# First block: the third query unit projected before the compressed keys' unit, and fewer weight units made ready at three early steps

## The chip, the cores and the metric

The program runs on one core of a Trainium2 chip. The metric is the device time of one execution in microseconds (us), as the median of several executions. The engines are TensorE (PE in the rows, its weight loads PEld), VectorE (DVE), ScalarE (ACT), GpSimd (POOL) and SyncE (SP), which issues nearly all DMAs.

## The reference

Two stacks of two layers each, on 256 tokens of width 1024. The change touches only the first stack, whose layer normalizes, projects into many pieces, runs three mixers, and then a feed-forward part:

```python
for l in range(DEPTH):
    h = rms_norm(x, ln1_gain[l])
    proj = h @ w_in[l]
    (nsa_q, k_cmp, v_cmp, k_slc, v_slc, k_win, v_win, nsa_gate,
     mla_cq, mla_ckv, mla_kpe, ret_q, ret_k, ret_v, ret_gate) = jnp.split(proj, offsets, axis=-1)
    o_nsa = nsa_mixer(partial_rope(nsa_q), partial_rope(k_cmp), v_cmp, partial_rope(k_slc), v_slc,
                      partial_rope(k_win), v_win, nsa_gate, ...)
    o_mla = mla_mixer(mla_cq, mla_ckv, mla_kpe, ...)
    o_ret = retention_mixer(ret_q, ret_k, ret_v, ret_gate, ...)
    x = x + concatenate([o_nsa, o_mla, o_ret]) @ w_out[l]
    x = x + square(relu(rms_norm(x, ln2_gain[l]) @ w_up[l])) @ w_down[l]
```

Inside `nsa_mixer` the compressed keys and values come from windows of 32 tokens, flattened and sent through a two-layer product: `kc = gelu((blocks(k_cmp) + pos_k) @ w1_k) @ w2_k`, and the same for values. Six query heads attend to selected keys, to a window of keys and to the compressed ones.

## The kernel before

All weights stream from HBM as tiles of 1 MB (128 x 2048 floats) through a ring of four slots (`ring`). SP issues the loads in one fixed order; before the load of tile g it waits until tile g-4, the one in the same slot, is released. Most tiles hold two weight units of 128 x 1024. A unit is split before use: ACT copies it to a rounded high part `wH` (L1305) and DVE subtracts to get the low part `wL` (L1648). A tile of units is released by the second subtraction. There are four places for split units, so unit n can be made only after TensorE is done with unit n-4. `feed(count)` on ACT and on DVE makes ready all units up to a count, in order, and each engine stops in it until the tile has landed (ACT) or the high part is there (DVE). A unit's projection is 24 matmuls (three for each of 8 chunks, L763 to L765).

A few tiles are used whole and unsplit: `cmpk` and `cmpv` (the first weights of the compression) and `small` (weights of the latent attention and the second ones of the compression). `cmpk` is released when TensorE ends `hidk`, its product (L944, 16 matmuls with 30 columns, each run as two passes, hence x32), and `cmpv` by `hidv`.

The tiles of a layer of the first block begin: 0 (cq0, cq1), 1 (ckv, q0), 2 (ks, q1), 3 and 4 token-major units, 5 (kc, q2), 6 cmpk, 7 (kw, vc), 8 (kpe, rqa), 9 cmpv, 10 small, 11 (rka, rqb), 12 (rkb, r4), 13 and 14 token-major, 15 the output product. The names are column groups of `w_in`: q0, q1, q2 the query heads in pairs, ks, kw, kc the selected, window and compressed keys, vc the compressed values, kpe and the r's for the other mixers. Unit numbers run along: kc 10, q2 11, kw 12, vc 13, kpe 14, rqa 15, rka 16, rqb 17, rkb 18, r4 19. So tile 10 (small) takes the slot of cmpk and can be loaded only when hidk has run, and tile 11 with units 16 and 17 is issued behind it in SP's order.

After the first units come 19 steps (`SLOTS1`), in which attention heads and projections alternate. Step i holds, on each engine, in this order:

- TensorE: projection `FILL1[i]`, with the rotations `MID1[i]` (L854) in its middle; on even i the scores of heads i and i+1 (L870, L872); the transposes of the weights of head i-1 (L885); the values of head i-2 (L893 to L895); then `END1[i]`: hidk, hidv, latent keys mk0 to mk4 (L974, from tile small), and so on.
- VectorE: rotary embeddings of `MID1[i]` (L1765 to L1771), behind kc's also four shifted copies and four additions of positions (L1873 to L1885), on which hidk waits; then `feed(fed_by(i))`; the row maxima of head i's scores (L1780); the output of head i-2 (L1922 to L1929).
- ScalarE: `feed(fed_by(i))`; the copy of the projection out of PSUM (L1253); the copy of the transposes (L1353); the copies of `END1[i]`'s results; the exponentials of head i (L1345, L1347).

Scores of heads 4 and 5 (step 4) need q2 after its rotary embedding, and the row maxima up to head 3. Scores of heads 6 and 7 (step 6) need the maxima up to head 5. The order is written out by hand in the tables `UNITS1`, `FILL1`, `MID1` and `END1`; `fed_by(i)` follows from which units' readers lie before step i and gives 16 at step 4, then 17, 18, 19, 20 at steps 5 to 8.

Of the kernel before, what the change touches and what calls it, by code (L numbers as in the profile page):

```python
# [45 lines left out]
assert KC * 256 == TILE  # L46


UNITS1 = ["cq0", "cq1", "ckv", "q0", "ks", "q1", "kc", "q2", "kw", "vc", "kpe", "rqa", "rka", "rqb", "rkb", "r4"]
RAW1 = {u: 6 + i if i < 3 else (i - 3) % 6 for i, u in enumerate(UNITS1)}  # L50
UNITS2 = [f"q{b}" for b in range(4)] + [f"k{b}" for b in range(4)]
LATER2 = ["pa", "pb", "cua", "cub", "cba", "cbb", "cca", "ccb"]
# [31 lines left out]

PAIRS1 = [(UNITS1[2 * i], UNITS1[2 * i + 1]) for i in range(8)]
TILES1 = (
# [92 lines left out]
def down_steps(kf):  # L179

    out = []
    for n in range(KC):
# [4 lines left out]
    return out  # L187


FILL1 = ["tm10", "tm11", "kc", "q2", "kw", "vc", "kpe", "rqa", "rka", "rqb", "rkb", "r4", "tm20", "tm21", "tm30", "tm31"]  # L190
SLOTS1 = NH1 + 2
MID1 = {3: ["kc"], 4: ["q2"], 5: ["kw"], 7: ["kpe"], 8: ["rqa"], 9: ["rka", "mq0"], 10: ["rqb", "mq1"],
        11: ["rkb", "mq2"], 12: ["r4", "mq3"], 13: ["mq4"]}
ROPES1 = ["q0", "ks", "q1"] + [u for i in range(SLOTS1) for u in MID1.get(i, [])]
END1 = {4: ["hidk"], 6: ["mk0", "mk1", "mk2"], 7: ["hidv", "mk3", "mk4"], 8: ["mv0", "mv1", "mq0"], 9: ["mq1", "mq2"],
        10: ["kcc", "mq3", "mq4", "vbd"], 11: ["cs0", "cs1"], 12: ["rs0", "rs1"],
        13: ["ct", "ro0", "ro1", "rs2", "rs3"], 14: ["co0", "co1", "ro2", "ro3", "rs4"], 15: ["ro4"],
        16: ["mt0", "mt1"], 17: ["mt2"]}
# [3 lines left out]
def fill1(i):  # L202

    return FILL1[i] if i < len(FILL1) else None


def fed_by(i):

    done = UNITS1[:6] + ["tm00", "tm01"] + FILL1[:i]
    n = SPLIT  # L210
    while n - SPLIT < 24 and SU1[n - SPLIT][2] in done:
        n += 1
    return min(n, 22) if i == 11 else n


SIDE = 3
# [2 lines left out]
def order1():  # L219

    out = UNITS1[:SIDE] + ["ss1", "q0", "rot_q0", "ks", "rot_ks", "q1", "ssqk", "rot_q1", "tm00", "tm01"]
    for i in range(SLOTS1):
        out += ["rot_" + u for u in MID1.get(i, [])]
        out += [fill1(i)] if fill1(i) else []
        out += END1.get(i, [])
    out += [f"wo{n}" for n in range(KC)]
# [82 lines left out]
def norm1(l, second):  # L309

    return 2 * l + second
# [87 lines left out]
def trn_kernel(nc, consts, vec1, vec2, once, pos, xin, stream, out):  # L399
    ctx = ExitStack()  # L400
    with ctx:
# [328 lines left out]
        def _(pe):  # L730
# [53 lines left out]
            def project_side_by_side(names, ready, y):  # L784

                chunk = side_by_side(names, y)
                for c in range(KC):
                    ready(c)
                    chunk(c)

            def normed(base):

                return lambda c: pe.wait_ge(h_ready, state["layer"] * (2 * KC) + (base + c + 1))

            def project(name, y, mid=None, ready=None):

                wh, wl = blocks(next_unit())
                a = open_acc(name)
                for c in range(KC):
                    if ready is not None:  # L800
                        ready(c)
                    if mid is not None and c == KC // 2:
                        mid()
                    last = split_product(a[:, 0:S], (wh[:, c, :], wl[:, c, :]), y(c), c == 0, c == KC - 1)
                last.then_inc(acc_full, 1)
# [31 lines left out]
            def sum_squares(name, norm):  # L837

                both = norm == norm2(0, 0)
                a = open_acc(name)  # L840
                pe.wait_ge(sum_ready, norm + 1)
                pe.matmul(a[:, 0:S], one[:], tcs[:, 0, :] if both else sq[:, 3, :], start=True, stop=False)
                pe.wait_ge(sq_ready, SQUARES * (norm + 1))
                pe.matmul(a[:, 0:S], g7[:] if both else one[:], sq[:, KC - 1, :], start=False, stop=True)\
                    .then_inc(acc_full, 1)
                if both:

                    pe.wait_ge(plain_ready, 1)
                    pe.matmul(ps_o[:, 0:S], one[:], sq[:, 3, :], start=True, stop=False)
                    pe.matmul(ps_o[:, 0:S], one[:], sq[:, KC - 1, :], start=False, stop=True).then_inc(plain_full, 1)  # L850
# [65 lines left out]
            for L in range(LAYERS):  # L916
                enter(A1, L)

                def rotated(u):

                    if u[:2] == "mq":
                        mla_rotate(int(u[2]))
                        return
                    drained(u)
                    i = RAW1[u]
                    if u == "kpe":
                        rotate(u, C("rotm")[0:96, 0:96], raw[0:96, i, :], slice(0, 96))
                    else:
                        rotate(u, C("rotr" if u[0] == "r" else "rotp"), raw[:, i, :])
# [136 lines left out]
                def after(i):  # L1066

                    for name in END1.get(i, []):
                        n = int(name[-1]) if name[-1].isdigit() else None
# [18 lines left out]
                def middle(i):  # L1088

                    for u in MID1.get(i, []):  # L1090
                        rotated(u)

                if L == 0:
                    for n, u in enumerate(UNITS1[:SIDE]):
                        project(u, hs, ready=normed(0) if n == 0 else None)
                    pe.wait_ge(one_ready, 1)
                    pe.wait_ge(early_in, 16 * 2)
                else:
                    project_side_by_side(UNITS1[:SIDE], normed(0), hs)
                sum_squares("ss1", norm1(L, 0))  # L1100
# [129 lines left out]
        def _(act):  # L1230
# [133 lines left out]
            for L in range(LAYERS):  # L1364
# [61 lines left out]
                def taken_after(i):  # L1426

                    for name in END1.get(i, []):
                        n = int(name[-1]) if name[-1].isdigit() else None
# [53 lines left out]
                for c in range(IN_TURN, HEADS_DONE):  # L1483
                    mixed_high(c)
                feed(fed_by(NH1))
                for c in range(HEADS_DONE, KC):
                    mixed_high(c)
# [90 lines left out]
        def _(dve):  # L1578
# [206 lines left out]
            for L in range(LAYERS):  # L1785
# [27 lines left out]
                def scaled(tables, by):  # L1813

                    n = len(range(4)[tables])
                    t = trig[:, :, tables, :]
                    link(TTN(t, t, by.unsqueeze(1).unsqueeze(1).to_broadcast([P, 2, n, S]), ALU.mult))
# [28 lines left out]
                def rope1_block(u):  # L1846

                    dve.wait_ge(acc_drained[A1.bank(u)], A1.drained(u, L))
                    allr = slice(0, P)
                    src = None if u[:2] == "mq" else raw[:, RAW1[u], :]  # L1850
                    done = L * len(ROPES1) + ROPES1.index(u) + 1
                    if u[:2] == "mq":
                        hh = int(u[2])
                        rope(A1, u, L, qm[64:96, hh, :], 1, [(qm[64:96, hh, :], slice(64, 96))], rope_ready, slice(64, 96))
                    elif u == "kpe":
                        rope(A1, u, L, src[64:96, :], 1, [(km[64:96, 0, :], slice(64, 96))], rope_ready, slice(64, 96))
                        dve.wait_ge(rope_ready, done)
                        nc.vector.tensor_copy(km[64:96, 1:5, :], km[64:96, 0:1, :].to_broadcast([32, 4, S]))\
                            .then_inc(km_ready, 1)
                    elif u == "kc":  # L1860
                        rope(A1, u, L, src, 0, [(nt, allr)], rope_ready)
                        dve.wait_ge(rope_ready, done)
                        shifted(nt, 0)
                    elif u == "r4":
                        rope(A1, u, L, src, 2, [(rope1[0:64, 9, :], slice(0, 64)), (rope1[0:64, 10, :], slice(64, 128))],
                             rope_ready)
                    else:
                        rope(A1, u, L, src, 2 if u[0] == "r" else 0, [(rope1[:, ROPE1[u], :], allr)], rope_ready)
# [197 lines left out]
                for i in range(SLOTS1):  # L2066
# [5 lines left out]
                    if (L, i) == (0, 7):  # L2072
                        dve.wait_ge(trig_ready, 4)
                        scaled(slice(2, 3), rn[:])
                    for u in MID1.get(i, []):
                        rope1_block(u)
                    if i == 6:
                        shifted(raw[:, RAW1["vc"], :], 1)
                    if i < NH1 - 1:
                        feed(fed_by(i))  # L2080
# [32 lines left out]
                    if i == 17:  # L2113
                        dve.wait_ge(o_drained, L * NH1 + (NH1 - 1) + 1)
                        dve.sem_inc(mla_ready, 1)
                    for name in END1.get(i, []):
                        if name[:2] == "mt":
# [383 lines left out]
```

## Time and profile before

| | |
|---|---|
| timed runs | 1563.92, 1570.98, 1573.01 us; median 1570.98 us |
| profiled execution | 1560.0 us, of which 1558.2 us are the span of the engines' work |
| PE busy | 1487.5 us, 95% of the span |
| DVE busy | 1086.7 us, 70% |
| ACT busy | 783.7 us, 50% |
| DMA | 296.51 MB, 190 GB/s on average |
| chain that ended last | PE 77%, DVE 12%, DMA 4%, ACT 3% |

The profile is of one execution. Its steps 0 to 18 of the first layer lie at about 45 to 190 us, of the second layer at about 417 to 545 us. A matmul row's idle time stands in brackets with the releaser. The granted clock of TensorE has two levels, 2.4 GHz (1.00) and 1.2 GHz (0.50); a mean in between is a stretch with both.

### The profile page before, as it was taken

What the parts mean: (1) busy time and instruction counts of PE and PEld (TensorE: products, weight loads), DVE (VectorE), ACT (ScalarE), POOL (GpSimd) and SP (SyncE); (2) the same over time, 40 slices, a digit from 0 to 9 for tenths busy, and PEclk for the clock granted to TensorE, in tenths of its full rate; (3) what the DMA queues carried; (4) which work ended last, traced back from release to release, by engine and by line L of the source; (5) the groups of instructions that cost most, each with busy time, mean ns of one, the idle gap of its engine ahead of it and who ended that gap; (6) DMA issues with size and microseconds to landing.
All of it is one profiled execution on the core that took longest, in us unless ns stands there. A gap on an engine that the chain in (4) does not pass through costs nothing.

```text
span 1558.2 us, 28765 instructions
## 1 busy us (share of the span) xinstructions
PE 1487.5 (95%) x11878; PEld 1444.9 (93%) x11878; DVE 1086.7 (70%) x1927; ACT 783.7 (50%) x1364; POOL 59.5 (4%) x61
## 2 busy tenths in 40 slices
PE   6899899999989899999899998999989999899999
PEld 5888899999988799999899988999989999799999
DVE  8658678888667678888985476666458746766653
ACT  6544567634534477733546545444435554454442
POOL 0000000000000000000030040000001202100000
PEclk9889999999999999999999999999999999999999
DMA  8123259898323149998544443555534444445552
GB/s 324 55 109 139 81 217 332 339 352 324 136 82 139 52 176 335 337 356 331 186 153 155 163 153 118 200 182 188 190 135 163 163 140 161 161 163 186 176 184 78
DMA packets 42433, 296.51 MB, mean 190 GB/s; under 512 B 5056, under 2 KB 5312, under 8 KB 6848
## 3 DMA queue, kind: packets, MB, share of 16 engines
q1 hardware_dynamic: 41888, 294.66, 51.5%
q8 instruction: 95, 1.56, 0.4%
q14 instruction: 34, 0.28, 0.1%
q10 hardware_dynamic: 416, 0.02, 0.0%
HBM read 293.61 MB, written 1.05 MB: 189 GB/s over the span
## 4 chain that ended last, share of the span: by engine, by line
PE 77%; DVE 12%; DMA 4%; ACT 3%; issue 2%; POOL 1%; SPq 0%; DVEq 0%; ACTq 0%
PE acc L763 23%; PE acc L765 22%; PE acc L764 22%; DVE wL L1648 4%; DMA ring<-stream 4%; ACT wH L1305 2%; PE acc L944 1%; PE ps_t L885 1%; PE acc L854 1%; PE ps_s L872 1%; PE ps_o L894 1%; PE ps_o L895 1%; PE ps_s L870 1%; PE acc L952 1%; POOL region L2361 1%
## 5 line engine op out<-in xcount | busy, mean ns | idle before, releaser
L1648 DVE TENSOR_TENSOR wL<-ring,wH 128x1024 fp32r<-128x1024 f32 x444 | 548.9, 1243 | 284.6 <-ACT wH L1305 279.7
L763 PE MATMUL acc<-hH,wH 128*128 128x256 f32 x2240 | 654.1, 292 | 33.6 <-DVE wL L1648 15.6
L764 PE MATMUL acc<-hL,wH 128*128 128x256 f32 x2240 | 639.0, 285 | 0.0
L765 PE MATMUL acc<-hH,wL 128*128 128x256 f32 x2240 | 638.8, 285 | 0.0
L1305 ACT ACTIVATE wH<-ring 128x1024 fp32r<-128x1024 f32 x444 | 463.7, 1051 | 229.7 <-DMA ring<-stream 118.1
L763 PEld LDWEIGHTS acc<-hH,wH 128*128 128x128 f32 x2240 | 435.2, 194 | 43.5 <-issue 25.5
L764 PEld LDWEIGHTS acc<-hL,wH 128*128 128x128 f32 x2240 | 435.4, 194 | 3.5 <-issue 2.6
L765 PEld LDWEIGHTS acc<-hH,wL 128*128 128x128 f32 x2240 | 434.9, 194 | 0.0
L763 PE MATMUL acc<-aH,wH 128*128 128x256 f32 x864 | 244.6, 283 | 0.0
L764 PE MATMUL acc<-aL,wH 128*128 128x256 f32 x864 | 244.5, 283 | 0.0
L765 PE MATMUL acc<-aH,wL 128*128 128x256 f32 x864 | 244.5, 283 | 0.0
L763 PEld LDWEIGHTS acc<-aH,wH 128*128 128x128 f32 x864 | 165.9, 192 | 0.1
L764 PEld LDWEIGHTS acc<-aL,wH 128*128 128x128 f32 x864 | 165.9, 192 | 0.0
L765 PEld LDWEIGHTS acc<-aH,wL 128*128 128x128 f32 x864 | 165.9, 192 | 0.0
L1253 ACT ACTIVATE region<-acc 128x256 f32<-128x256 f32 (+4 forms) x142 | 53.7, 379 | 192.5 <-PE acc L765 159.1
L1638 DVE SCALAR_TENSOR_TENSOR ring<-ring,onc 128x1024 f32<-128x1024 f32 x96 | 117.0, 1219 | 0.4 <-DMA ring<-stream 0.4
L763 PE MATMUL acc<-wH,hH 128*128 128x256 f32 (+1 forms) x192 | 58.3, 304 | 3.7 <-DVE tss L1767 1.5
L1780 DVE CUSTOM_DVE_ANT_0 weights<-ps_s,cst 128x128 f32<-128x128 f32 x100 | 31.3, 354 | 34.8 <-PE ps_s L872 34.4
L764 PE MATMUL acc<-wL,hH 128*128 128x256 f32 (+1 forms) x192 | 54.4, 283 | 0.0
L765 PE MATMUL acc<-wH,hL 128*128 128x256 f32 (+1 forms) x192 | 54.4, 283 | 0.0
L2348 POOL TENSOR_TENSOR region<-region 128x256 f32<-128x256 f32 x12 | 13.2, 1100 | 1069.8 <-ACT region L1253 1068.8
L763 PEld LDWEIGHTS acc<-wH,hH 128*128 128x128 f32 x192 | 37.1, 193 | 7.6 <-issue 4.3
(312 smaller groups left out, 1699.9 us busy)
## 6 DMA issues: line engine op xcount, KB each, us to landing
ring<-stream SPq DMA_DIRECT2D x276, 1024.0 KB, 4.9
cst<-consts SPq DMA_DIRECT2D x1, 1347.0 KB, 16.0
x<-xin SPq DMA_DIRECT2D x4, 256.0 KB, 3.8
out<-x SPq DMA_DIRECT2D x4, 256.0 KB, 4.2
onc<-once SPq DMA_DIRECT2D x1, 516.0 KB, 16.2
v1all<-vec SPq DMA_DIRECT2D x1, 355.0 KB, 9.7
v2all<-vec SPq DMA_DIRECT2D x1, 330.0 KB, 17.0
nv<-pos SPq DMA_DIRECT2D x1, 256.0 KB, 3.5
```

The lines of the kernel that those rows point to most:

```text
L763: pe.matmul(out, w[0], y[0], start=first, stop=False)
L764: pe.matmul(out, w[0], y[1], start=False, stop=False)
L765: return pe.matmul(out, w[1], y[0], start=False, stop=last)
L854: pe.matmul(a[rows, 0:S], m, src, start=True, stop=True).then_inc(acc_full, 1)
L870: pe.matmul(b[:, 0:P], q[:, 0:P], k[:, 0:P], start=True, stop=True)
L872: pe.matmul(b[:, P:3 * P], q[:, P:S], k, start=True, stop=True).then_inc(s_full, 1)
L885: last = pe.transpose(ps_t[:, c * P:(c + 1) * P], pr[:, j % 2, c * P:(c + 1) * P], C("ident"))
L1253: act.activation(dst, a[rows, 0:n], func, **kw).then_inc(acc_drained[tn.bank(name)], 1)
L1305: act.activation(wH[:, n % SPLIT, :], ring[:, g % RING, half * UNIT:(half + 1) * UNIT], ACT.Copy)\
L1638: STT(products, products, 1.0, cb2, ALU.mult, ALU.mult, accum_out=adac[:, 2 * j + half:2 * j + half + 1])\
L1648: TTN(wL[:, n % SPLIT, :], ring[:, g % RING, half * UNIT:(half + 1) * UNIT], wH[:, n % SPLIT, :].bitcast(F32), ALU.subtract).then_inc(lo_r ...
L1780: last = nc.vector.tensor_tensor_reduce(sm[:, i % 2, cols], ps_s[i % 2][:, cols], C("mask")[:, cols], -scale, FLT_MAX, ALU.add, ALU.min, n ...
```

## The change

Three tables swap q2 and kc, and hidk goes from the end of step 4 to the end of step 5. The two units change halves in tile 5 and their numbers (q2 is unit 10, kc unit 11). DVE now makes q2's rotary embedding at step 3 and kc's with its copies at step 4. `fed_by` is capped at steps 5, 6 and 7, so that unit 16 isn't made at step 5 nor unit 17 at step 6, but both at step 7; steps 4 and 8 and the later ones reach the same counts as before. Nothing is added to or removed from the work.

```diff
-UNITS1 = ["cq0", "cq1", "ckv", "q0", "ks", "q1", "kc", "q2", "kw", "vc", ...]
+UNITS1 = ["cq0", "cq1", "ckv", "q0", "ks", "q1", "q2", "kc", "kw", "vc", ...]
...
-FILL1 = ["tm10", "tm11", "kc", "q2", "kw", ...]
+FILL1 = ["tm10", "tm11", "q2", "kc", "kw", ...]
...
-MID1 = {3: ["kc"], 4: ["q2"], 5: ["kw"], ...}
+MID1 = {3: ["q2"], 4: ["kc"], 5: ["kw"], ...}
...
-END1 = {4: ["hidk"], 6: ["mk0", "mk1", "mk2"], ...}
+END1 = {5: ["hidk"], 6: ["mk0", "mk1", "mk2"], ...}
...
+FED_AT_MOST = {5: 16, 6: 16, 7: 18, 11: 22}
...
-    return min(n, 22) if i == 11 else n
+    return min(n, FED_AT_MOST.get(i, n))
```

Lines of the changed program lie 3 further on. VectorE, from step 3's rotary embedding on (first layer), before: kc's embedding (into `nt`), copies and additions, then the unit's split.

```order
L1765 TENSOR_TENSOR tcs<-region,trig 128x256
L1767 TENSOR_TENSOR tss<-acc,trig 128x256
L1771 TENSOR_TENSOR nt<-tcs,tss 128x256
L1873 COPY region<-nt 64x256
L1874 COPY region<-nt 64x255
L1875 COPY region<-nt 64x255
L1876 COPY region<-nt 64x256
L1884 TENSOR_TENSOR region<-region,v1all 128x8x15
L1885 TENSOR_TENSOR region<-region,v1all 128x8x15
L1884 TENSOR_TENSOR region<-region,v1all 128x8x15
L1885 TENSOR_TENSOR region<-region,v1all 128x8x15
L1648 TENSOR_TENSOR wL<-ring,wH 128x1024
```

The same place in the changed program: q2's embedding, the split, head 3's maxima (L1783), head 1's output, and then kc's embedding.

```order
L1768 TENSOR_TENSOR tcs<-region,trig 128x256
L1770 TENSOR_TENSOR tss<-acc,trig 128x256
L1774 TENSOR_TENSOR region<-tcs,tss 128x256
L1651 TENSOR_TENSOR wL<-ring,wH 128x1024
L1783 ISA weights,nmax<-ps_s,cst 128x128
L1783 ISA nmax 128x1
L1783 ISA weights,nmax<-ps_s,cst 128x256
L1783 ISA nmax 128x1
L1925 RECIPROCAL coef<-psumv 128x2
L1928 TENSOR_TENSOR coef<-coef,region 128x2
L1932 TENSOR_TENSOR region<-ps_o,coef 128x2x64
L1768 TENSOR_TENSOR tcs<-region,trig 128x256
```

The eight copies and additions moved behind step 3's maxima and output, and behind q2's embedding.

ScalarE from the end of step 4 on, before: hidk's copy (128x30), head 4's exponentials, the split of unit 16, then step 5's transposed copy and exponentials, the split of unit 17, step 6's copies.

```order
L1253 ACTIVATE region<-acc 128x30
L1345 ACTIVATE weights,psumv<-weights,nmax 128x128
L1347 ACTIVATE weights,psumv<-weights,nmax 128x256
L1305 ACTIVATE wH<-ring 128x1024
L1353 ACTIVATE weights<-ps_t 128x384
L1345 ACTIVATE weights,psumv<-weights,nmax 128x128
L1347 ACTIVATE weights,psumv<-weights,nmax 128x256
L1305 ACTIVATE wH<-ring 128x1024
L1353 ACTIVATE weights<-ps_t 128x384
L1253 ACTIVATE region<-acc 64x256 x3
```

The same stretch in the changed program, from head 4's exponentials to step 7's split of two units:

```order
L1348 ACTIVATE weights,psumv<-weights,nmax 128x128
L1350 ACTIVATE weights,psumv<-weights,nmax 128x256
L1356 ACTIVATE weights<-ps_t 128x384
L1256 ACTIVATE region<-acc 128x30
L1348 ACTIVATE weights,psumv<-weights,nmax 128x128
L1350 ACTIVATE weights,psumv<-weights,nmax 128x256
L1356 ACTIVATE weights<-ps_t 128x384
L1256 ACTIVATE region<-acc 64x256 x3
L1348 ACTIVATE weights,psumv<-weights,nmax 128x128
L1350 ACTIVATE weights,psumv<-weights,nmax 128x256
L1308 ACTIVATE wH<-ring 128x1024 x2
```

hidk's copy went one step later, and both splits to step 7, behind step 6's exponentials.

## Rows read from the trace of the kernel before

**Rows 1.** The page: TensorE's busy time, and the chain that ended last by engine.

```profile
PE 1487.5 (95%) x11878; PEld 1444.9 (93%) x11878; DVE 1086.7 (70%) x1927; ACT 783.7 (50%) x1364; POOL 59.5 (4%) x61
PE 77%; DVE 12%; DMA 4%; ACT 3%; issue 2%; POOL 1%; SPq 0%; DVEq 0%; ACTq 0%
```

**Rows 2.** The chain in order of time, first layer: start, duration, what.

```profile
61.67 0.42 DVE tcs L1765
...
62.92 0.28 DVE region L1873
...
65.32 1.13 DVE wL L1648
66.45 0.20 DVE weights L1780
...
67.11 0.17 DVE coef L1925
...
67.60 0.33 DVE tcs L1765
...
78.37 0.33 SPq L695
...
85.64 1.07 ACT wH L1305
```

**Rows 3.** Timeline of TensorE, first layer: start, duration, form, idle time and releaser.

```profile
68.78 0.49 PE L870 MATMUL ps_s<-region 64*128 64x128 f32 x4 [2.44 <-DVE region L1771]
...
71.36 6.98 PE L944 MATMUL acc<-region,ring 128*128 128x30 f32 x32
...
88.66 0.49 PE L870 MATMUL ps_s<-region 64*128 64x128 f32 x4 [0.68 <-DVE nmax L1780]
...
90.68 1.51 PE L974 MATMUL acc<-region,ring 128*64 128x256 f32 x6
...
94.60 0.64 PE L854 MATMUL acc<-region,cst 96*96 96x256 f32 x2 [0.78 <-DVE region L1842]
```

**Rows 4.** Stretches, first layer: PE, PEld, DVE, ACT, POOL busy, granted clock, DMA.

```profile
66.00:71.40 5.40, 2.96 (x21) 2.43 (x20) 4.64 (x18) 2.69 (x7) 0.00 (x0) 0.86 0.00 0
71.40:78.20 6.80, 6.80 (x34) 6.80 (x33) 0.62 (x2) 0.00 (x0) 0.00 (x0) 0.50 0.00 0
78.20:86.00 7.80, 7.80 (x45) 7.62 (x46) 0.85 (x2) 1.44 (x6) 0.00 (x0) 0.66 0.87 327
...
97.50:104.00 6.50, 6.50 (x40) 5.28 (x39) 2.50 (x9) 1.08 (x5) 0.00 (x0) 0.74 0.19 53
104.00:110.00 6.00, 6.00 (x39) 5.36 (x37) 2.23 (x6) 2.12 (x6) 0.00 (x0) 0.72 0.30 122
```

**Rows 5.** Timeline of TensorE, second layer.

```profile
438.44 0.49 PE L870 MATMUL ps_s<-region 64*128 64x128 f32 x4 [1.09 <-DVE region L1771]
...
440.30 3.71 PE L944 MATMUL acc<-region,ring 128*128 128x30 f32 x32
443.84 0.37 PE L763 MATMUL acc<-hH,wH 128*128 128x256 f32 x1
...
448.14 0.37 PE L763 MATMUL acc<-hH,wH 128*128 128x256 f32 x1
...
454.33 0.49 PE L870 MATMUL ps_s<-region 64*128 64x128 f32 x4 [3.07 <-DVE nmax L1780]
...
463.76 3.71 PE L944 MATMUL acc<-region,ring 128*128 128x30 f32 x32
```

**Rows 6.** Stretches, second layer, columns as in rows 4.

```profile
454.00:460.00 6.00, 5.67 (x28) 4.01 (x29) 5.75 (x23) 3.56 (x10) 0.00 (x0) 0.72 0.00 0
```

**Rows 7.** Timeline of ScalarE: exponentials, first layer; the split of unit 16, second layer.

```profile
67.44 0.49 ACT L1347 ACTIVATE weights<-weights,nmax 128x256 f32<-128x256 f32 x1
...
451.31 1.06 ACT L1305 ACTIVATE wH<-ring 128x1024 fp32r<-128x1024 f32 x1 [6.20 <-DMA ring<-stream]
```

**Rows 8.** Line L695 (loads) from 76 to 90 us, three loads: issue to landing.

```profile
DMA to landing us min/median/max: 4.7/6.9/10.3
```

More of the change, by code:

```diff
@@ L46 @@
 assert KC * 256 == TILE
-UNITS1 = ["cq0", "cq1", "ckv", "q0", "ks", "q1", "kc", "q2", "kw", "vc", "kpe", "rqa", "rka", "rqb", "rkb", "r4"]
+UNITS1 = ["cq0", "cq1", "ckv", "q0", "ks", "q1", "q2", "kc", "kw", "vc", "kpe", "rqa", "rka", "rqb", "rkb", "r4"]
 RAW1 = {u: 6 + i if i < 3 else (i - 3) % 6 for i, u in enumerate(UNITS1)}
@@ L187, in down_steps @@
     return out
-FILL1 = ["tm10", "tm11", "kc", "q2", "kw", "vc", "kpe", "rqa", "rka", "rqb", "rkb", "r4", "tm20", "tm21", "tm30", "tm31"]
+FILL1 = ["tm10", "tm11", "q2", "kc", "kw", "vc", "kpe", "rqa", "rka", "rqb", "rkb", "r4", "tm20", "tm21", "tm30", "tm31"]
 SLOTS1 = NH1 + 2
-MID1 = {3: ["kc"], 4: ["q2"], 5: ["kw"], 7: ["kpe"], 8: ["rqa"], 9: ["rka", "mq0"], 10: ["rqb", "mq1"],
+MID1 = {3: ["q2"], 4: ["kc"], 5: ["kw"], 7: ["kpe"], 8: ["rqa"], 9: ["rka", "mq0"], 10: ["rqb", "mq1"],
         11: ["rkb", "mq2"], 12: ["r4", "mq3"], 13: ["mq4"]}
 ROPES1 = ["q0", "ks", "q1"] + [u for i in range(SLOTS1) for u in MID1.get(i, [])]
-END1 = {4: ["hidk"], 6: ["mk0", "mk1", "mk2"], 7: ["hidv", "mk3", "mk4"], 8: ["mv0", "mv1", "mq0"], 9: ["mq1", "mq2"],
+END1 = {5: ["hidk"], 6: ["mk0", "mk1", "mk2"], 7: ["hidv", "mk3", "mk4"], 8: ["mv0", "mv1", "mq0"], 9: ["mq1", "mq2"],
         10: ["kcc", "mq3", "mq4", "vbd"], 11: ["cs0", "cs1"], 12: ["rs0", "rs1"],
```

## The prediction

> **What bounds the kernel now.** I first read the page. TensorE is busy for 95% of the span and holds 77% of the chain that ended last [rows 1], so nearly everything else is hidden. A change in order can only give back what TensorE loses: time in which it stands still, and time in which it runs at the lower clock. So I looked in TensorE's timeline at steps 3 to 8 of both layers for the idle times in brackets, and in the stretches for the granted clock.
>
> First layer. At step 4 TensorE stands still for 2.44 us before the scores of heads 4 and 5, released by q2's rotary embedding [rows 3]. The chain shows why that is late: VectorE makes kc's embedding from 61.67, its copies and additions from 62.92, the split from 65.32, head 3's maxima from 66.45 and head 1's output from 67.11, and begins q2's embedding only at 67.60 [rows 2]. After this stop the clock is at 1.2 GHz for some 14 us: the product hidk takes 6.98 us [rows 3], where in the second layer, at 2.4 GHz, it takes 3.71 [rows 5]. When hidk ends at 78.37, SP issues the load of small and behind it that of tile 11; ScalarE, at step 5's split of unit 16, stands until tile 11 has landed, 85.64 [rows 2]. The maxima of head 5 wait behind that, and TensorE waits 0.68 us for them, then 0.78 for the next VectorE result [rows 3]. That is short only since the slow clock stretched its own work. A second stretch at the lower clock lies at 97.5 to 110 [rows 4].
>
> Second layer. The same two places: 1.09 us for q2, without a fall of the clock behind it, and 3.07 us for head 5's maxima [rows 5], behind a split that waited 6.20 us for its tile [rows 7]; then the clock fell [rows 6].
>
> **What the change moves, part by part.** The work is the same; I walk through the steps with its measured lengths.
>
> *q2 before kc.* VectorE's pieces are: an embedding 62.92 - 61.67 = 1.25 us, copies and additions 65.32 - 62.92 = 2.40, split 1.13, maxima 67.11 - 66.45 = 0.66, output 67.60 - 67.11 = 0.49 [rows 2]. New order from 61.67: q2 embedded at 62.92, split 64.05, head 3's maxima 64.71, output 65.20. TensorE asks for the scores at 68.78 - 2.44 = 66.34, and both of their conditions are met by 64.71. The stall is gone, with 1.6 us to spare. In the second layer it asks 1.09 us before 438.44, and q2's embedding moves up there by as much as here, 67.60 - 61.67 = 5.9 us. Gain 2.44 + 1.09.
>
> *What is late next on VectorE.* kc's embedding and copies now stand ahead of head 4's maxima: 65.20 + 1.25 + 2.40 + 1.13 + 0.66 = 70.64, and the exponentials on ScalarE end 67.44 + 0.49 - 67.11 = 0.82 us behind their maxima [rows 7], at 71.5. TensorE: scores, transposes and values take 440.30 - 438.44 = 1.86 us [rows 5], so vc's projection starts at 66.34 + 1.86 = 68.20. A whole odd step (projection with rotation, transposes, values) takes 448.14 - 443.84 = 4.30; I estimate transposes and values at half of the 1.86, 0.9 us, so it wants head 4's weights at 68.20 + 3.4 = 71.6. That is a tie: I take 0, and 0.3 us as the bound. Kc's additions are done at 68.85, long before hidk.
>
> *hidk one step later.* It starts at 68.20 + 4.30 = 72.50 and, at the full clock, ends at 72.50 + 443.84 - 440.30 = 76.04, where before it ended at 78.37. In the second layer it ends 3.0 us later than before (437.35 + 1.86 + 4.30 + 3.54 = 447.05, against 444.04), but with vc's step already behind it.
>
> *The small tile.* This is the new danger. The three latent keys at the end of step 6 read tile small, which now has one step less to land. After hidk TensorE has kpe's projection, 454.33 - 3.07 - 448.14 = 3.12 us, then scores, transposes and values, 1.86: 4.98 us in all. The first of the three loads landed 4.7 us after its issue [rows 8], and SP issues it at once. So the tile is there 0.2 us early: cost 0. The bound above is the landing of the second load, 6.9, which would be 2 us in each layer.
>
> *Units 16 and 17 at step 7.* ScalarE and VectorE no longer stop at step 5 for tile 11, so head 5's maxima are made early, and the stops of 0.68 and 3.07 us go; VectorE also has vc's and kpe's copies out of PSUM in time, so 0.78 goes. At step 7 ScalarE gets to the split at about 4.98 + 1.5 (mk0 to mk2 [rows 3]) = 6.5 us after hidk's end and may wait until 6.9 + 0.3; TensorE needs unit 16 only at step 8, that is after an odd step's 4.3, hidv's 3.7 [rows 5] and two latent keys' 1.0, some 9 us on. Two splits in step 7 and two in step 8 hold VectorE for 2.3 us each. Cost 0, hidden under hidv; without that cover it would be one split, 1.13 us.
>
> *The clock.* What a stretch loses is its length times (1 - clock). First layer, the fall after the first stop: 5.40 x 0.14 + 6.80 x 0.50 + 7.80 x 0.34 = 6.81 us; the second one: 6.50 x 0.26 + 6.00 x 0.28 = 3.37 us [rows 4]. Second layer: 6.00 x 0.28 = 1.68 us [rows 6]. The first and the third stand right behind a stop of 2.44 and 3.07 us that goes away, so I count them as gained. The second stands in and behind hidv, whose matmuls have only 30 columns, after stops of 0.68 and 0.78 us. The hidv of the second layer shows no fall. The trace doesn't decide it: I leave this fall where it is, and keep 0 and 3.37 as ends.
>
> The Trainium skill (TensorE: Matmul & The Clock Gate, Part 1) says that the check behind the clock runs freely and isn't tied to the kernel's start, so that the point of a change varies from run to run. Of the three such products that began at the full clock, one had a fall and two had none, which agrees. That rule makes the rival below on falls at each of these products.
>
> **The sum.** First layer 2.44 + 0.68 + 0.78 + 6.81 = 10.71; second layer 1.09 + 3.07 + 1.68 = 5.84; together 16.55 us, all of it on TensorE's own path. Later work moves up with it, since every load waits for a slot and not for a point in time. Against the profiled execution: 1560.0 - 16.6 = 1543.4. That execution is 11 us under the median of the timed runs, so the forecast is set against the median: 1570.98 - 16.55 = **1554.4 us**. The gap may be falls of the clock that the profiled execution was spared, for instance behind the stop of 1.09; then the gain is larger.
>
> **Rivals.** *All falls go* (0.20): the fall at hidv goes with the stops before it, 16.55 + 3.37 = 19.9 us, 1551.1. For it: the undisturbed hidv of the second layer.
>
> *Falls at the narrow products* (0.20): hidk now runs at the full clock in both layers and may pull it down, as hidv did. If all four do so at 3.37 us each, the gain is 19.9 - 13.5 = 6.4 us, 1564.6; with two or three, 1558 to 1561. Against it: two of the three that began at the full clock have no fall, and the one in the first layer had two stops before it.
>
> *Only the swap works* (0.05): the block on ScalarE shows up again at step 7 and TensorE stops for it as at step 6 before. What is left is the gain of step 4, 2.44 + 1.09 + 6.81 = 10.3 us, 1560.6. Against it: the 9 us of work that lie between.
>
> *small is late by 2 us* (0.07): it lands as the second load did. That is a stop of 1.9 us in each layer and, as after 2.44 us before, one fall of 6.8: 16.55 - 3.8 - 6.8 = 5.9, 1565.1.
>
> *Slower* (0.03): the three loads issued together share the engines so that small lands last, at 10.3 [rows 8]. TensorE then stops 5.3 us in each layer, with a fall of 6.8 behind it: 16.55 - 24.2 = -7.7, 1578.7. It turns to a loss when stop and fall together pass 8.3 us a layer. Against it: in the rows the first load lands first.
>
> The Trainium skill (DMA: Bandwidth & Descriptors, Queues, rings and completion order) says that completion isn't first-in first-out for one issuing engine, which is the rule by which this rival would come about. The landings of 4.7, 6.9 and 10.3 us do not show it.
>
> **Chances and range.** The forecast itself has 0.45. Half a per cent, 7.9 us, is about what a measurement of this kernel can tell from no change. Under 1563.1 lie the forecast, the first rival, 0.14 of the second and most of the third: faster 0.84. The rest is within (0.13), and 0.03 slower. The range goes from the best case, 1551.1, less 5 us for the scatter of the timed runs (9 us between lowest and highest), to the second rival's end: 1546 to 1565.
>
> **What would show it.** In the changed kernel's rows: no idle time before the scores of step 4 in either layer; hidk 3.7 us long in both; no wait of ScalarE for its tile at step 5; at most some tenths before mk0 (L977, then with DMA as releaser); mk0 starting near 81.0 in the first layer instead of 90.68, and in the second hidv starting 10.7 + 5.8 = 16.5 us earlier than 463.76. A stop at step 5's transposes would mean that kc's chain is too long for its new place; a stop at mk0 that small is the new bound; a clock of 0.50 behind hidk without a stop, the second rival.

## The result

Seven executions of each kernel on one chip gave a median of 1549.04 us for the changed kernel (1544.11 to 1550.31) and 1559.62 us for the kernel before (1557.81 to 1573.01; the three shown ahead of the prediction are among them). The ratio is 0.9898, 95% interval 0.9875 to 0.9921: faster by 1.0%, 10.6 us. The profiled execution of the changed kernel took 1549.25 us, 10.8 us less than the profiled one of before. The forecast was a gain of 16.6 us and a time of 1554.4 us. One of the ten executions of the swap alone, a variant further down, took 3661.84 us and is in none of its figures.

TensorE's timeline of the changed kernel, first layer from step 4 to the latent keys (start, duration, form; an idle time would stand in brackets at the end):

```profile
67.14 0.49 PE L873 MATMUL ps_s<-region 64*128 64x128 f32 x4
...
72.55 0.52 PE L888 MATMUL ps_t<-cst,weights 128*128 128x128 f32 x3
...
73.53 4.98 PE L947 MATMUL acc<-region,ring 128*128 128x30 f32 x32
...
83.22 0.49 PE L873 MATMUL ps_s<-region 64*128 64x128 f32 x4
...
85.17 1.51 PE L977 MATMUL acc<-region,ring 128*64 128x256 f32 x6
...
90.95 3.71 PE L947 MATMUL acc<-region,ring 128*128 128x30 f32 x32
```

None of the stops of [rows 3] is left. The scores of step 4 follow without one, those of step 6 (83.22) too, and the latent keys (85.17, before 90.68) find their tile. Step 5's transposes (72.55) carry no bracket; they start 0.3 us behind the start of the matmul ahead of them, against 0.1 us in the second layer, so the tie cost 0.2 us at most. But hidk, forecast at 3.7 us in this view, takes 4.98. The second layer shows the same:

```profile
428.67 0.49 PE L873 MATMUL ps_s<-region 64*128 64x128 f32 x4
...
434.83 4.53 PE L947 MATMUL acc<-region,ring 128*128 128x30 f32 x32
...
444.50 0.49 PE L873 MATMUL ps_s<-region 64*128 64x128 f32 x4
...
452.23 3.71 PE L947 MATMUL acc<-region,ring 128*128 128x30 f32 x32
```

The stops of 1.09 and 3.07 us of [rows 5] are gone. The stretches say what happened to hidk (PE, PEld, DVE, ACT, POOL busy, granted clock, DMA share, GB/s):

```profile
66.00:75.70 9.70, 9.66 (x83) 8.97 (x81) 9.31 (x35) 3.65 (x10) 0.00 (x0) 1.00 0.00 0
75.70:82.50 6.80, 6.80 (x33) 6.80 (x33) 1.15 (x5) 1.06 (x5) 0.00 (x0) 0.50 0.43 154
...
434.00:437.50 3.50, 3.50 (x35) 3.50 (x33) 3.15 (x15) 0.49 (x1) 0.00 (x0) 1.00 0.02 5
437.50:444.30 6.80, 6.80 (x34) 6.80 (x33) 0.63 (x3) 1.06 (x5) 0.00 (x0) 0.50 0.59 204
```

TensorE was busy for all but 0.04 us of the stretch before, and yet the clock fell to 1.2 GHz within hidk (at 75.7 and 437.5 us), in both layers, for 6.8 us each: half of that, 3.4 us a layer, was lost. Of the falls of before [rows 4, 6], the one behind the first stop and the one at hidv are gone, as is the one of the second layer's step 6.

Two further stretches fell in this execution that had not in the one of before. Where the second layer starts, TensorE waits a little shorter than before (2.04 us, before 2.58), and the clock falls:

```profile
378.32 0.36 PE L766 MATMUL acc<-hH,wH 128*128 128x256 f32 x1 [2.04 <-DVE tss L2176]
```

At the start of the second block it falls at 744.7 us, behind a stop of 2.66 us that is the same in both kernels. Both kernels reach this stop with the same work, so I count this fall as chance and not as the change's.

### The profile page after: what moved, and what is told of

Read it like the earlier page. It is cut to its first block, busy times and chain, and to the rows that moved or that the text cites. A ratio compares the mean times of both kernels' runs of the same rounds, so it can differ in the third digit from the quotient of the medians.

```text
span 1547.4 us, 28765 instructions
## 1 busy us (share of the span) xinstructions
PE 1483.0 (96%) x11878; PEld 1441.1 (93%) x11878; DVE 1085.8 (70%) x1927; ACT 780.0 (50%) x1364; POOL 59.4 (4%) x61
## 4 chain that ended last, share of the span: by engine, by line
PE 68%; DVE 14%; DMA 10%; ACT 4%; issue 2%; POOL 1%; SPq 0%; DVEq 0%; ACTq 0%
PE acc L766 20%; PE acc L768 19%; PE acc L767 19%; DMA ring<-stream 10%; DVE wL L1651 6%; ACT wH L1308 3%; DVE ring L1641 2%; PE ps_t L888 1%; PE acc L947 1%; PE acc L857 1%; PE ps_s L875 1%; PE ps_o L897 1%; PE ps_o L898 1%; PE ps_s L873 1%; PE acc L955 1%
## 5 line engine op out<-in xcount | busy, mean ns | idle before, releaser
L1308 ACT ACTIVATE wH<-ring 128x1024 fp32r<-128x1024 f32 x444 | 461.7, 1050 | 232.3 <-DMA ring<-stream 130.6
L1783 DVE CUSTOM_DVE_ANT_0 weights<-ps_s,cst 128x128 f32<-128x128 f32 x100 | 31.3, 353 | 48.8 <-PE ps_s L875 48.4
```

The costliest lines, as they stand in the source:

```text
L1308: act.activation(wH[:, n % SPLIT, :], ring[:, g % RING, half * UNIT:(half + 1) * UNIT], ACT.Copy)\
L1783: last = nc.vector.tensor_tensor_reduce(sm[:, i % 2, cols], ps_s[i % 2][:, cols], C("mask")[:, cols], -scale, FLT_MAX, ALU.add, ALU.min, n ...
```

## The experiments

Four kernels ran on a second chip and four on a third, each time beside the kernel before. On those the kernel before has medians of 1566.9 us (29 executions, 1554 to 1577) and 1567.9 us (25 executions, 1555 to 1574). Each execution comes with its mean granted clock, so its time splits into lost clock, (1 - mean clock) x span, and the rest. (A stop that falls into a stretch at 1.2 GHz is put down by this to lost clock with half its length.) For the kernel before on the third chip that is 31.3 us lost and 1535.1 us rest on average; time and lost clock go together over its executions (correlation 0.82). By the scatter of these 25 (a standard deviation of 4.7 us), a median of three can lie 5 us off, by my estimate. Unless a 95% interval of a ratio is given, the intervals below are estimates from such standard deviations.

### Wider matmuls for hidk and hidv

```diff
+flat_f = fk[j].rearrange("p m g n -> p (m g n)")
 for m in range(16):
-    last = pe.matmul(a[:, 0:30], tl[:, m, :], fk[j][:, m, :, :].rearrange("p g n -> p (g n)"),
+    n = min(120, 480 - 30 * m)
+    last = pe.matmul(a[:, 0:n], tl[:, m, :], flat_f[:, 30 * m:30 * m + n],
                      start=m == 0, stop=m == 15)
```

`flat_f` is the same tile seen as 480 columns. The first 30 columns of the result are what they were; the others aren't read.

> The changed kernel, but each of the 16 matmuls of hidk and hidv streams 120 columns of the same tile in place of 30 (90, 60, 30 for the last three); the first 30 results are the same. Theory (the new falls of the clock at 75.7 and 437.5 us come from the narrow matmuls of hidk): both falls go, hidk takes 3.6 us in both layers, the matmuls take no longer since their weight load sets the pace, and the profiled execution is 2 x 3.4 = 6.8 us shorter than 1549.2, near 1542.5. Rival (the falls come from stops elsewhere, or hit whatever runs when the check comes): the falls stay, the time stays at 1549.

```profile
66.00:75.70 9.70, 9.68 (x82) 8.98 (x81) 9.27 (x35) 3.44 (x10) 0.00 (x0) 1.00 0.00 0
75.70:82.50 6.80, 6.63 (x56) 5.95 (x55) 2.33 (x12) 1.56 (x6) 0.00 (x0) 1.00 0.66 233
434.00:437.50 3.50, 3.50 (x34) 3.50 (x33) 2.96 (x11) 0.03 (x1) 0.00 (x0) 1.00 0.00 0
437.50:444.30 6.80, 6.80 (x52) 5.56 (x52) 1.92 (x9) 2.55 (x9) 0.00 (x0) 1.00 0.78 308
```

These are the same stretches in this kernel, all at the full clock. The matmuls take no longer, and the small tile is now, as forecast, on the edge:

```profile
73.31 3.71 PE L949 MATMUL acc<-region,ring 128*128 128x120 f32 x32
82.09 1.48 PE L979 MATMUL acc<-region,ring 128*64 128x256 f32 x6 [0.17 <-DMA ring<-stream]
```

Its median was 1547.7 us, ratio 0.9877 to the kernel before (0.9839 to 0.9916), with 1544.9 us in the profiled execution, 2.4 us more than expected. The expectation took away only the two falls of hidk; this profile has one fall elsewhere less (at 379.5 us) and one more (at about 123 us), so the 2.4 us aren't clock, and what they are stays open. One profile without a fall could be chance, so it ran again beside the changed kernel, on the third chip.

> The changed kernel with 120 columns in hidk and hidv, beside the changed kernel. Theory (narrow matmuls pull the clock): its mean granted clock is higher by 6.8 us of lost time in each execution that would have had both falls, so 3 to 7 us under the changed kernel. Rival (the missing falls turn up elsewhere, or the wide matmuls cost the same in another way): no difference over 2 us.

> The changed kernel, on one chip with the next three. Theory (16.6 us forecast, of which the profile of the changed kernel shows the stops gone, and 3.4 us given back at hidk in each layer): 10 to 17 us under the kernel before, by medians. Rival (the first comparison's 10.6 us is all there is): 9 to 12 us.

| third chip | executions | median us | ratio to before (95%) | lost clock us | rest us |
|---|---|---|---|---|---|
| before | 25 | 1567.9 | 1 | 31.3 | 1535.1 |
| changed | 8 | 1555.8 | 0.9926 (0.9900 to 0.9952) | 27.8 | 1527.3 |
| changed, 120 columns | 6 | 1546.1 | 0.9869 (0.9839 to 0.9899) | 19.0 | 1526.6 |

The changed kernel gains 12.0 us here by medians, 11.3 by means. That lies in both ranges given ahead of the run (10 to 17 and 9 to 12), so it doesn't tell them apart. Of the means, 7.8 us are in the rest (an interval of some 2.5 us each way), close to the five stops of the forecast (2.44 + 0.68 + 0.78 + 1.09 + 3.07 = 8.1 us). Only 3.5 us (also some 3.5 each way) come from the clock, where the forecast had 8.5. The wide matmuls give 8.7 us more clock (some 4 each way) and leave the rest as it is: a further 9.7 us by medians, and the fastest version of this study. The 3 to 7 us expected lie partly within that interval. The falls are not always those of the first profile: in the changed kernel's profile on this chip both hidk ran at the full clock, but the clock fell just behind hidv:

```profile
72.97 3.71 PE L947 MATMUL acc<-region,ring 128*128 128x30 f32 x32
...
87.36 3.71 PE L947 MATMUL acc<-region,ring 128*128 128x30 f32 x32
```

and the stretch behind the second of them:

```profile
91.50:95.50 4.00, 4.00 (x18) 3.38 (x17) 0.00 (x0) 3.52 (x8) 0.00 (x0) 0.57 0.72 262
```

So which of the products takes the fall varies from one execution to another. All ten profiles of this study, the one of before and those of the variants below among them, can be asked the same: of the products hidk and hidv that began at the full clock, how many had the clock fall while they ran or within 0.8 us of their end?

| profile | began at the full clock | clock fell within | just behind |
|---|---|---|---|
| before | 3 | 1 | 0 |
| changed | 4 | 2 | 0 |
| changed, third chip | 4 | 0 | 1 |
| caps alone | 4 | 1 | 3 |
| caps and hidk at step 5 | 4 | 1 | 2 |
| swap alone | 4 | 3 | 0 |
| changed without caps | 4 | 3 | 0 |
| all with 30 columns | 27 | 11 | 6 |
| the three with 120 columns | 11 | 0 | 0 |

17 of 27 with 30 columns, none of 11 with 120. Five of the 17 also had a stop of 0.5 to 2.4 us in the 4 us ahead of the product; the other 12 had none. So the narrow matmuls bring falls, and the rival that the missing falls would turn up elsewhere is out.

### The same in the kernel before

> The kernel before, with the same 120 columns in hidk and hidv. Theory (narrow matmuls pull the clock at hidv, the stop of 2.44 us pulls it before hidk): the fall at 100.6 us goes (3.4 us), the fall at 69.8 us behind the stop stays, though it may be one half shorter since hidk keeps TensorE fuller (another 3.4 us): 1553 to 1557. Rival (only stops pull the clock): the fall at 100.6 comes again, 1560.

It came out at 1564.6 us, ratio 0.9984 (0.9956 to 1.0011), 27.2 us of lost clock against 29.6 and the same rest, 1536.8 us: no gain clear of noise, and less than the 3 to 7 us expected. What was expected of the two products did come: no fall at hidv, and the fall behind the stop of step 4 lasts 3.4 us instead of 13.7 (68.9 to 72.3). But the profile shows a loss in another place:

```profile
68.76 0.73 PE L870 MATMUL ps_s<-region 64*128 64x128 f32 x4 [2.42 <-DVE region L1773]
...
72.15 3.78 PE L946 MATMUL acc<-region,ring 128*128 128x120 f32 x32
...
87.73 0.80 PE L870 MATMUL ps_s<-region 64*128 64x128 f32 x4 [4.55 <-DVE nmax L1782]
...
97.79 3.71 PE L946 MATMUL acc<-region,ring 128*128 128x120 f32 x32
```

hidk is now fast, so TensorE is ready sooner at step 6 and stops there for 4.55 us where [rows 3] have 0.68, and the clock is at 1.2 GHz behind that: the scores take 0.80 us where 0.49 is the full pace, and the stretch from 87 to 91 us shows it.

```profile
87.00:91.00 4.00, 3.27 (x17) 2.65 (x17) 3.82 (x18) 2.42 (x6) 0.00 (x0) 0.50 0.00 0
```

In this execution what the faster hidk won went into the stop and the fall behind it. The 0.68 us of the first layer were that short in a profile whose hidk ran at the lower clock, as the prediction says; with hidk at the full clock the same stop is 4.55 us here and 3.07 in the second layer of before. That this is so on average is not shown: the rest of the 12 executions is not longer than before's.

### The parts one by one

The caps alone, in the kernel before:

```diff
-    return min(n, 22) if i == 11 else n
+    return min(n, {5: 16, 6: 16, 7: 18, 11: 22}.get(i, n))
```

> The kernel before with the caps alone; hidk stays at step 4, kc ahead of q2. Theory (what stops TensorE at step 6 is ScalarE's stand at step 5 for tile 11, so taking unit 16 away from there removes it, wherever hidk is): the stops of 0.68 and 3.07 us go, as in the kernel with hidk at step 5, and time is within 2 us of that kernel (6 to 11 us under the kernel before). Rival (hidk must move too): no gain.

Median 1556.4 us, ratio 0.9937 (0.9912 to 0.9961): 11.4 us by medians, nearly the whole change, and at the upper end of the 6 to 11 us expected. Lost clock 28.9, rest 1527.9 us. The stop at step 6 is gone with hidk still at step 4; that at step 4 stays:

```profile
68.61 0.49 PE L870 MATMUL ps_s<-region 64*128 64x128 f32 x4 [2.40 <-DVE region L1771]
...
70.47 3.71 PE L944 MATMUL acc<-region,ring 128*128 128x30 f32 x32
```

The caps and hidk at step 5, kc still ahead of q2 (on the second chip):

```diff
-END1 = {4: ["hidk"], ...}
+END1 = {5: ["hidk"], ...}
...
-    return min(n, 22) if i == 11 else n
+    return min(n, {5: 16, 6: 16, 7: 18, 11: 22}.get(i, n))
```

> The kernel before with hidk at step 5 and the caps, but kc still ahead of q2. Theory (the swap is worth the stops of 2.44 and 1.09 us and the 6.8 us of the fall behind the first; hidk and the caps are worth the stops at step 6): the stops of step 4 stay, those of 0.68 and 3.07 us are gone, and the profiled execution lies near 1560 - 0.7 - 0.8 - 3.1 = 1555.4, within 3.4 us for each fall that comes or goes. Rival (moving hidk and the splits is all that counts): 1549, as the whole change.

Median 1556.2 us, ratio 0.9933 (0.9899 to 0.9967); lost clock 26.0 against 29.6 of before there, rest 1530.0 against 1536.8. The profiled execution took 1555.2 us, where 1555.4 were expected; that a single execution hits so closely is partly luck. The two ratios can't be told apart, so moving hidk adds nothing measurable to the caps. Its rest is 6.8 us under the kernel before, and that of the caps alone 7.2, each with an interval of some 2.6 us each way: more than the 4.5 us that the stops of step 6 and 7 add up to in the rows, but just within noise of it. It could be that the stop of the first layer is 3 us or more in executions in which the clock holds. That isn't shown, and the whole change, whose rest fell by no more than 7.8 us, speaks against it.

The swap alone:

```diff
-FED_AT_MOST = {5: 16, 6: 16, 7: 18, 11: 22}
+FED_AT_MOST = {11: 22}
...
-END1 = {5: ["hidk"], ...}
+END1 = {4: ["hidk"], ...}
```

> The changed kernel with hidk back at step 4 and no caps. Theory: the scores of step 4 have no stop, but hidk then waits for kc's additions, done at 69.5 us in the changed kernel, where TensorE is ready at about 69.0: at most 1 us; the stop at step 6 behind tile 11 stays, so the gain is that of the swap alone, 3.5 us and the 6.8 us of the fall behind it: 3 to 10 us under the kernel before. Rival (the swap alone only moves the stop of 2.4 us to hidk): no gain.

Median of nine executions 1558.1 us, ratio 0.9957 (0.9931 to 0.9982): 9.7 us by medians, by the ratio 3 to 11 us, where 3 to 10 were expected. The rest is 1531.5 us, 3.6 under the kernel before; lost clock is 4.0 us lower.

```profile
68.83 5.08 PE L947 MATMUL acc<-region,ring 128*128 128x30 f32 x32 [0.51 <-issue]
...
84.36 0.49 PE L873 MATMUL ps_s<-region 64*128 64x128 f32 x4 [1.39 <-DVE nmax L1783]
```

The stop of 2.44 us went, hidk waits half a microsecond in its old place, and the stop of step 6 stays: 1.39 us here, 0.95 in the second layer. The 3.6 us of the rest look like the 3.53 us of the two stops of step 4, but they are made otherwise: the five bracketed stops that its profile has at these steps of the two layers (0.51, 1.39, 0.82, 0.95, 0.79 us) add up to 4.5 us, against 8.1 before. So either part alone is worth most of the whole: by medians 9.7 + 11.4 = 21.1 us against 12.0 together. In the rest the parts are 3.6 + 7.2 = 10.8 against 7.8, in lost clock 4.0 + 2.4 = 6.4 against 3.5. The intervals (some 4 us each way for a ratio) leave open how much of that gap is real; in the stops of the profiles the parts do add up, 3.6 + 4.5 = 8.1 us.

The whole change without its caps:

```diff
-FED_AT_MOST = {5: 16, 6: 16, 7: 18, 11: 22}
+FED_AT_MOST = {11: 22}
```

> The changed kernel without the caps at steps 5 to 7. Theory (the caps keep ScalarE from standing at step 5 for tile 11): ScalarE stands from about 73 us until 7.3 us after hidk's end, the maxima of head 5 come 10.3 us after hidk's end where TensorE wants them after 3.1, so it stops some 7 us in each layer (5 us where hidk's fall slows it) with a fall behind it: 1549 + 2 x (6 to 10) = 1561 to 1569. Rival (the caps are idle, since nothing waits for unit 16 that early): 1549.

Median 1574.0 us, ratio 1.0043 (1.0011 to 1.0076): slower than the kernel before. By the ratios it is 1.2%, 18 us, over the changed kernel, within the 12 to 20 us expected. ScalarE's timeline:

```profile
84.71 1.06 ACT L1308 ACTIVATE wH<-ring 128x1024 fp32r<-128x1024 f32 x1 [12.45 <-DMA ring<-stream]
```

and TensorE's:

```profile
87.73 0.80 PE L873 MATMUL ps_s<-region 64*128 64x128 f32 x4 [6.07 <-DVE nmax L1783]
...
458.17 0.80 PE L873 MATMUL ps_s<-region 64*128 64x128 f32 x4 [7.39 <-DVE nmax L1783]
```

ScalarE stands 12.45 us at step 5's split, since the load of tile 11 now waits for a hidk that comes a step later. TensorE stops 6.07 and 7.39 us for it, where some 7 were expected, and in both layers the clock is at 1.2 GHz for over 10 us around and behind the stop (83.8 to 94.0 and 455.8 to 466.1 us). On average the whole loss is in lost clock, 37.7 us against 29.6; the rest is 1535.5 against 1536.8, though these two stops add up to 13.5 us and the five of before to 8.1. Some 6 us of the stops lie in stretches at 1.2 GHz, so 3 us of them are counted as lost clock; why the rest doesn't rise by the remainder is open. With hidk at step 5 the caps are what makes the move bearable.

### What scatters beside the clock

Not all of the time between two executions of the changed kernel is clock. TensorE's waits for the splits of the feed-forward weights' tiles differ too. The list of waits (us in total, times, longest), first the profile on the first chip:

```profile
PE acc L766 <- DVE wL L1651: 17.8, 6, 14.7
```

and that on the third:

```profile
PE acc L766 <- DVE wL L1651: 23.8, 15, 14.2
```

That is 23.8 - 17.8 = 6.0 us more in 15 waits instead of 6. The longest of each is the start of the program; of the others, 12 in the second profile and two in the first lie in the feed-forward parts. The change does not touch these parts. ScalarE's waits for its tiles to land are longer too in the second profile (143.6 us against 130.6); why was not tried.

## Why the prediction was right or wrong

*What bounds the kernel, and the stops.* Right, all five. The stops of 2.44, 1.09, 0.68, 0.78 and 3.07 us are gone from the changed profile, and the rest without lost clock fell by 7.8 us on the third chip against 8.1 summed. That it is so close is partly luck, with an interval of some 2.5 us each way.

*What is late next on VectorE.* Right: step 5's transposes lose 0.2 us at most, the tie that was called, within its bound of 0.3.

*The small tile.* Right in the changed kernel, no wait. The latent keys start at 85.17 us, not near 81.0, since hidk and what follows it ran at the lower clock; in the third chip's profile, where hidk kept the full clock, they start at 81.61. With 120 columns 0.17 us of wait appear, where 0.2 us of slack were worked out.

*Units 16 and 17 at step 7.* Right. Without the caps the same move makes the kernel 1.2% slower (ratio 1.0043 against 0.9926 with them, on different chips, each against the kernel before on its own).

*hidk one step later.* Its start was right (73.5 with an execution that began 0.9 us later than the one of before; 72.50 was worked out). "At the full clock" was wrong in the profile of the result, where it took 4.98 and 4.53 us; in the third chip's profile both took 3.71.

*The clock, the first of two steps that failed.* The sum's term for the clock was 6.81 + 1.68 = 8.5 us. It counted the falls behind stops as a gain and put at nothing that the products, once they run at the full clock, bring falls of their own. That was the second rival, given 0.20; two of its four falls came in the profiled execution, and the wide matmuls show that they come from the narrow matmuls. What the term measured is 3.5 us on average on the third chip, and 3.4 us between the two profiled executions of the first. The account of the two profiled executions: 16.55 forecast, less 2 x 3.4 for hidk, less 2 x 1.7 for the falls at 379.5 and 744.7 us, less 0.9 us of a later start, plus 3.4 for the fall at hidv that the forecast had kept, plus 1.7 for one at 134.7 us that is gone, is 10.6 us, against 10.8 measured. Waits of half a microsecond and less that differ in other places are not in it, so the last tenths are luck.

*The base, the second step that failed.* The gain was set against the median of three executions, 1570.98 us, and not against the profiled 1560.0, which was taken for one that had been spared some falls. On that chip the median of seven was 1559.62 us: the profiled execution was an ordinary one, and the three were high. Why they were is open, since no clock is on record for them. From the profiled execution the forecast would have been 1543.4, 5.6 under the measured time; from the median it came out 5.4 over it. So 1554.4 us was near only by luck, because a base 11 us too high met a gain 6 us too large, and against the median of seven it says 5.2 us of gain where 10.6 were measured.

*Rivals.* The slower one (small landing last) did not come: the three loads landed within 4.7 to 8.8 us of their issue. The prediction had small as the first of them, though [rows 8] give no order; the kernel with 120 columns bears it out, where the latent keys, released by small's landing, start at 82.09 us, 5.1 us behind hidk's end. "Only the swap works" is refuted by the caps alone. "All falls go" did not come either: in the changed kernel's profile two fell at hidk.

## What to carry to other kernels

A split or copy that is made ready ahead stops its whole engine when its tile hasn't landed; look for such a wait ahead of short work that the bottleneck needs, and cap the look-ahead there before moving anything else. Set a sum against a base of many executions and keep the two parts apart, stops and lost clock: the stops can be summed from the rows (8.1 us here, 7.8 measured, with 2.5 us of noise), the clock has to be forecast for the new order, in which busy but narrow stretches can be followed by falls as the old stops were. Where a matmul takes no longer with more columns, stream more columns through it and ignore what they give. It cost nothing here and, on top of the reordering, was worth nearly as much as the reordering itself; in the kernel before it was worth nothing that could be told from noise.

## What the runs showed of the hardware

- TensorE's clock fell to 1.2 GHz though TensorE had been busy for 9.66 of the 9.70 us before (66.0 to 75.7 us), during matmuls with 30 moving columns. Over all profiles it fell in or just behind 17 of 27 such products that began at 2.4 GHz, and in or behind none of 11 with 120 columns and the same busy time. The Trainium skill (TensorE: Matmul & The Clock Gate, Part 1) says that the gate follows how busy the engine has been; here the busy time in the rows did not tell whether the clock would hold.
- 32 fp32 matmul records with their weight loads took the same 3.71 us with 30 columns as with 120 (90, 60 and 30 for the last three of the 16 pairs), both at 2.4 GHz.
- Behind equal stops the clock did not always do the same: nine of the ten profiles have the stop of 2.66 us at the start of the second block at the full clock. It fell right behind it in seven and held in two (before, swap alone).
